# Two transformer blocks on one core: rotary rotations by transfers of rows instead of matmuls, and the mixers' rotation arithmetic on GpSimd

## The chip, the cores and the metric

One core of one Trainium2 chip. The metric is device microseconds of one execution. The engines are TensorE (PE), VectorE (DVE), ScalarE (ACT), GpSimd (POOL) and SyncE (SP), which issues most of the DMAs.

## What is computed

Two programs follow one another on a sequence of 256 tokens with 1024 features, both two layers deep and in fp32. The first block is a vision block with a context stream of another 256 tokens; the second ("mixer") has three kinds of attention between two feed-forward parts. Both turn some of their query and key rows by rotary angles:

```python
def apply_rope(x, cos, sin):            # first block: pairs (2i, 2i+1)
    x0, x1 = xf[..., 0], xf[..., 1]
    out = jnp.stack([x0 * cos - x1 * sin, x0 * sin + x1 * cos], axis=-1)

def partial_rope(x, cos, sin):          # mixer: rows i and i+8 of each head's first 16
    r1 = (x1 * c - x2 * s).astype(x.dtype)
    r2 = (x2 * c + x1 * s).astype(x.dtype)
    return jnp.concatenate([r1, r2, x[..., ROPE_DIM:]], axis=-1)
```

In the first block the grouped queries (8 heads) and keys are turned after their norm. In the mixer it is the 5 query heads of the selecting attention (`q_c`), its key `k_c`, the 4 index queries `q_i` and the index key `k_i`.

## The kernel before

Features lie on the 128 partitions, tokens along the free dimension. Each product of an activation with a weight is made of three fp32r matmuls (high part by high part, low by high, high by low). The weights come in 330-odd **pieces** of up to 1 MB through a ring of four buffers. ACT writes a piece's high part (`w_hi`, line 1750), DVE subtracts it to the low part in place (`ring_lo`, line 2267, called by `ahead`), PE reads both (lines 1258, 1301, 1395, 1504). Each function that adds to the plan appends an item to one list, and each engine walks this list in order and does what it has in every item; no engine changes its order at run time.

SP issues the pieces in order. Piece n goes out as soon as PE has begun piece n-3:

```python
if p.n >= RING:
    sp.wait_ge(piece_begun, p.n - RING + 2)
```

A rotation is an item `rope`. PE multiplies the chunk of 128 rows (64 for the index key and for the last query head) by a fixed matrix `rot1` or `rot2` of 0, 1 and -1 into a PSUM bank (line 1548, fp32). DVE then makes the product of that with the sine (line 2635), of the chunk with the cosine (line 2636) and the sum (line 2638), which raises `rope_ready`. Those who need it wait for this semaphore: PE's scores of the grouped and of the selecting attention (`pe_att`), PE's index scores (`pe_index`, line 1679), ACT's copies of keys (lines 1977, 2077).

There are 24 rotations, numbered through: 1 to 5 in layer 0 of the first block, 6 to 10 in its layer 1, then 7 in each layer of the mixer. In layer 0 of the first block the list alternates steps of attention (`att`), chunks of gate weights (`gates`) and pieces of the modulation weights (`mod`, line 1410). An attention step is: scores into the two S banks (line 1572), softmax on DVE out of these banks (line 2668; reciprocal line 2680), exponentials on ACT, the product with the reciprocal on POOL (line 2184), transposes on PE (line 1585), copies, values (line 1600). Half of the steps stand in the middle of a chunk's matmuls (`mids`). The scores of the next step wait until DVE has emptied both S banks. The head norm (`head_sums`, `head_spread`, DVE line 2624) precedes the rotations. In layer 0 rotation 3 stands between `head_spread` of the last chunk (pieces 23 and 24 just before it) and the attention step ahead of piece 25.

In the mixer the rotations stand among the matmuls of pieces 188 to 190 (layer 0) and 301 to 303 (layer 1), and the index scores among those of the piece after (`2f`, chunk 10).

## Time and profile before

| | |
|---|---|
| median of 3 runs | 2416.3 us (2415.94 to 2416.79) |
| the profiled execution | 2416.34 us |
| its span, first to last instruction | 2414.5 us |
| PE busy | 2393.6 us, 99% of the span |
| DVE, ACT, POOL busy | 64%, 51%, 17% |
| mean granted clock of PE | 0.999 |

A busy share is an average over stages. Rows of a timeline give start and length in us; the length of a matmul overlaps that of its neighbours, so the spacing of starts tells what one costs. Line numbers are those of the kernel before. "<-" in brackets names what ended the idle time before an instruction.

### The profile page before, as it was taken

The page shows a single profiled execution, that of the slowest core. Times are in us where ns is not written, and L with a number is a line of the kernel's source. Part 1 is how long each engine was busy: PE and PEld are TensorE (multiplying, and loading weights), DVE is VectorE, ACT ScalarE, POOL GpSimd, SP SyncE. Part 2 cuts the span into 40 slices and gives each one's busy share as a digit, 9 for nine tenths or more (in the row PEclk, how much of TensorE's full clock was granted, in tenths as well). Part 3 has the DMA queues.
Part 4 walks back from the last instruction along what each step waited for, and adds up shares of the span by engine and source line. Part 5 has one row for each costly group of instructions (what it writes and reads, how often), then busy time and mean ns, then how long its engine had stood idle before and what let it go on. Part 6 is the DMA issues. An engine that isn't in the chain of part 4 may idle for free.

```text
span 2414.5 us, 36498 instructions
## 1 busy us (share of the span) xinstructions
PE 2393.6 (99%) x14216; PEld 2036.5 (84%) x14216; DVE 1538.3 (64%) x2659; ACT 1219.4 (51%) x2268; POOL 405.0 (17%) x388
## 2 busy tenths in 40 slices
PE   8999999999999999999999999999999999999998
PEld 6766689888888877988888899898888889989887
DVE  5335455663455555677677777677767767767775
ACT  4344444322222546565565545665556554566554
POOL 0343322000001335100100100540010010154000
PEclk9999999999999999999999999999999999999999
DMA  6334423453444422455565553355565564436554
GB/s 280 132 114 158 157 88 122 159 169 135 157 165 141 157 89 95 150 192 176 194 212 181 172 184 128 123 193 192 170 208 180 176 195 151 151 112 200 190 175 137
DMA packets 88602, 389.92 MB, mean 161 GB/s; under 512 B 15024, under 2 KB 27600, under 8 KB 58352
## 3 DMA queue, kind: packets, MB, share of 16 engines
q1 hardware_dynamic: 81232, 356.07, 43.4%
q0 software_dynamic: 7200, 31.52, 3.8%
q8 instruction: 114, 1.87, 0.3%
q14 instruction: 56, 0.46, 0.1%
HBM read 386.52 MB, written 1.05 MB: 161 GB/s over the span
## 4 chain that ended last, share of the span: by engine, by line
PE 93%; DVE 3%; ACT 2%; POOL 1%; issue 1%; DMA 0%; DVEq 0%; SPq 0%; POOLq 0%; ACTq 0%
PE ps L1301 42%; PE ps L1258 38%; PE ps L1504 3%; PE ps L1572 2%; PE ps L1585 2%; PE ps L1600 2%; DVE ring_lo L2267 1%; PE ps L1395 1%; ACT logits L1989 1%; ACT w_hi L1750 1%; PE ps L1410 1%; POOL logits L2184 1%; PE ps L1548 1%; DMA x_res<-xt 0%; PE ps L1429 0%
## 5 line engine op out<-in xcount | busy, mean ns | idle before, releaser
L2267 DVE TENSOR_TENSOR ring_lo<-ring,w_hi 128x1024 fp32r<-128x1024 f32 (+4 forms) x708 | 781.8, 1129 | 200.1 <-ACT w_hi L1750 199.0
L1750 ACT ACTIVATE w_hi<-ring 128x1024 fp32r<-128x1024 f32 (+4 forms) x708 | 633.4, 944 | 280.1 <-PE ps L1258 186.7
L1301 PE MATMUL ps<-h_hi,w_hi 128*128 128x512 f32 x2144 | 527.2, 393 | 0.6 <-DVE h_hi L2440 0.3
L1301 PEld LDWEIGHTS ps<-h_hi,w_hi 128*128 128x128 f32 x2144 | 391.3, 188 | 76.6 <-issue 2.5
L1258 PE MATMUL ps<-h_hi,w_hi 128*128 128x256 f32 (+1 forms) x1520 | 410.6, 333 | 2.0 <-ACT arena L1879 1.2
L1258 PE MATMUL ps<-h_lo,w_hi 128*128 128x512 f32 (+1 forms) x976 | 325.5, 351 | 0.0
L1301 PEld LDWEIGHTS ps<-h_hi,ring_lo 128*128 128x128 f32 x2144 | 281.3, 191 | 14.5 <-DVE ring_lo L2267 0.9
L1301 PE MATMUL ps<-h_hi,ring_lo 128*128 128x256 f32 x2144 | 288.2, 282 | 0.0
L1258 PEld LDWEIGHTS ps<-h_hi,w_hi 128*128 128x128 f32 x1520 | 252.3, 190 | 37.6 <-issue 11.2
L1258 PE MATMUL ps<-h_hi,ring_lo 128*128 128x256 f32 (+1 forms) x1248 | 253.3, 338 | 0.3 <-DVE ring_lo L2267 0.3
L2509 DVE TENSOR_TENSOR prob_t<-ps,prob_t 128x256 f32<-128x256 f32 x260 | 109.7, 422 | 196.3 <-ACT prob_t L1902 196.0
L2140 POOL TENSOR_TENSOR logits<-logits 128x256 f32<-128x256 f32 (+1 forms) x65 | 67.6, 1040 | 991.0 <-ACT logits L1771 776.5
L1301 PE MATMUL ps<-hid_both,w_hi 128*128 128x512 f32 x880 | 226.2, 392 | 0.0
L1258 PEld LDWEIGHTS ps<-h_hi,ring_lo 128*128 128x128 f32 x1248 | 200.8, 189 | 28.4 <-issue 2.2
L2184 POOL TENSOR_SCALAR logits<-logits,stat 128x512 f32<-128x512 f32 (+2 forms) x140 | 167.9, 1211 | 261.4 <-DVE stat L2680 261.2
L1902 ACT ACTIVATE prob_t<-ps 128x256 f32<-128x256 f32 x260 | 98.1, 377 | 220.6 <-PE ps L1301 220.3
L1258 PEld LDWEIGHTS ps<-h_lo,w_hi 128*128 128x128 f32 x976 | 182.3, 189 | 23.5 <-DVE h_lo L2440 0.2
L1301 PEld LDWEIGHTS ps<-hid_both,w_hi 128*128 128x128 f32 x880 | 160.8, 188 | 30.9
L1989 ACT ACTIVATE logits<-logits,stat 128x512 f32<-128x512 f32 (+2 forms) x140 | 81.6, 584 | 140.4 <-DVE logits L2668 85.5
L1301 PE MATMUL ps<-hid_both,ring_lo 128*128 128x256 f32 x880 | 133.4, 282 | 0.0
L1301 PEld LDWEIGHTS ps<-hid_both,ring_lo 128*128 128x128 f32 x880 | 122.4, 191 | 5.7
L1928 ACT ACTIVATE prob_t<-prob_t 128x256 f32<-128x256 f32 x110 | 46.0, 418 | 105.3 <-DVE prob_t L2533 93.5
(301 smaller groups left out, 2934.0 us busy)
## 6 DMA issues: line engine op xcount, KB each, us to landing
ring<-w_ffn_in SPq DMA_DIRECT2D x132, 1024.0 KB, 4.9
ring<-w_ffn_out SPq DMA_DIRECT2D x96, 704.0 KB, 4.0
ring<-w_in SPq DMA_DIRECT2D x36, 1024.0 KB, 4.9
ring<-w_w_in SPq DMA_DIRECT2D x26, 1024.0 KB, 5.0
bias_t<-w_mod POOLq DMA_DIRECT2D x24, 1024.0 KB, 5.4
ring<-w_mod SPq DMA_DIRECT2D x16, 1024.0 KB, 6.0
ring<-w_up SPq DMA_DIRECT2D x16, 576.0 KB, 3.8
ring<-w_pab SPq DMA_DIRECT2D x8, 1024.0 KB, 4.9
```

Source lines behind the costliest of these rows:

```text
L1258: mm = pe.matmul(ps[fs[k].bank][:, at_col:at_col + n], (hi_w if wpart == "hi" else lo_w)[0:rows, at[k]:at[k] + P], hi if part == "hi" else ...
L1301: mm = pe.matmul(ps[f.bank][:, 0:cols], wt[:, at + q * P:at + q * P + P], both[:, 0:cols], start=left[q] == n, stop=left[q] == 1, skip_gro ...
L1504: mm = pe.matmul(ps[f.bank][:, 0:st["n"]], rows, wt[:, at:at + st["n"]], start=c == 0 and part == 0 and not low, stop=c == KC - 1 and low)
L1572: mm = pe.matmul(ps[f.bank][:, s2["at"]:s2["at"] + s2["nk"]], p["q"][a, s2["t"] * P:(s2["t"] + 1) * P], p["k"][a, k0:k0 + s2["nk"]], start ...
L1585: mm = pe.transpose(ps[f.bank][:, c * P:(c + 1) * P], logits[:, o:o + P], ident)
L1750: act.activation(w_hi[q.s % 2][:, h * n:(h + 1) * n], ring[q.slot][:, h * n:(h + 1) * n], ACT.Copy)\
L1902: act.activation(tmp[i][:, S:SQ], ps[f.bank][:, S:SQ], ACT.Copy).then_inc(half_out, 1)
L1989: act.activation(lg, lg, ACT.Exp, scale=-1.0, bias=stat[:, o:o + 1], accum_out=stat[:, 4 + o:5 + o])\
L2140: pool.tensor_tensor(sq_sum[:, o:n], sq_sum[:, o:n], sq[j % 2][:, o:n], ALU.add).then_inc(sq_added, 1)
L2184: pool.tensor_scalar(lg, lg, stat[:, 8 + (a % 2) * 2 + h:9 + (a % 2) * 2 + h], None, ALU.mult)\
L2267: dve.tensor_tensor(ring_lo[q.slot][:, c], ring[q.slot][:, c], plain(w_hi[q.s % 2][:, c]), ALU.subtract)\
L2509: dve.tensor_tensor(tmp[i][:, to:to + S], ps[f.bank][:, 0:S], tmp[i][:, S:SQ], ALU.add).then_inc(psum_taken[f.bank], 1)
```

## The change

The matrices `rot1` and `rot2` and all 24 matmuls go. In their place SP copies the partner rows of a chunk into a buffer (`turned_by`, `turned_by2`, two halves each) by DMA, from SBUF to SBUF: in the first block two transfers of 64 rows with a step of two, in the mixer two transfers of 8 rows for each head. The signs are in the sine table now. Each swap stands in SP's stream behind the load of a given piece (`plan.swaps`), waits until its chunk is written and until the rotation two before is done, since that one used the same half. The arithmetic stays on DVE in the first block, with a wait for the transfers; in the mixer it is on POOL, three operations with a wait between. In layer 1 of the first block and in the mixer the items have moved in the list too. `swap_clear` zeroes `turned_by2` once on DVE.

```diff
@@ -85,27 +85,20 @@
...
-    put("rot1", rot)
-    put("sin1", np.sin(ang).T[pair])
+    put("sin1", np.sin(ang).T[pair] * np.where(p % 2, 1, -1)[:, None])
-    put("rot2", rot)
...
-            sin[a] = sin[b] = np.sin(ang[i])
+            sin[a], sin[b] = -np.sin(ang[i]), np.sin(ang[i])
@@ -627,9 +623,20 @@
-        def rope(chunks, block, need=(), inside=False, bank=None):
-            return add("rope", block=block, need=need, tb=turned_by if block == 1 else turned_by2, inside=inside,
-                       chunks=[(b, a, low, fill(T_BANKS[i % 2] if bank is None else bank) if bank or not inside else linear(), count("rope")) for i, (b, a, low) in enumerate(chunks)])
+        def swap(chunk, block, need, later=0):
+
+            buf, at, low = chunk
+            n = count("swap")
+            moves = 2 if block == 1 or low else 4
+            t = dict(buf=buf, at=at, low=low, block=block, need=need, n=n, tb=turned_by if block == 1 else turned_by2,
+                     landed=count(f"swap_landed{n % 2}", 16 * moves))
+            plan.swaps.setdefault(len(plan.pieces) + 2 + later, []).append(t)
+            return t
+
+        def rope(*turns):
+            for t in turns:
+                count("rope")
+                add("rope" if t["block"] == 1 else "rope2", t=t, part=count("rope_part", 2) if t["block"] == 2 else None)
 
         def head_norm(chunks, root, kv=False, low=(0,) * 5):
@@ -831,12 +842,14 @@
                 some(unit, 2)
                 two_steps()
                 head_spread(hn, 0, 1)
+                turned = swaps(0, 1)
                 some(unit, 2)
                 two_steps()
                 head_spread(hn, 2, 3)
                 some(unit, 2)
                 two_steps(last=False)
-                rope(ropes[:2], 1, need=(hn["spread"][1],))
+                rope(*turned)
+                turned = swaps(2, 3, later=2)
                 add("keys_swap", n=1)
                 turn(unit)
                 unit = held_unit(2)
@@ -845,11 +858,12 @@
                 two_steps()
                 some(unit, 2)
                 head_spread(hn, 4)
-                rope(ropes[2:3], 1, need=(hn["spread"][2],), bank=T_BANKS[1])
+                rope(turned[0])
+                turned += swaps(4, later=1)
                 two_steps(last=False)
-                rope(ropes[3:4], 1, need=(hn["spread"][3],))
+                rope(turned[1])
                 two_steps()
-                rope(ropes[4:5], 1, need=(hn["spread"][4],))
+                rope(turned[2])
                 for _ in range(3):
                     some(unit, 2)
                     two_steps(last=False)
@@ -878,21 +892,25 @@
                 head_sums(hn)
                 next(nk[1])
                 head_spread(hn, 0, 1)
+                turned = swaps(0, 1)
                 g = attention([dict(na_pair(0, 0, 0, SQ), after=(feats["naq", 0], feats["nak", 0]))])
                 att(g)
                 run_all(nk[1])
                 head_spread(hn, 2, 3)
+                rope(*turned)
                 vals = values()
                 att(g)
+                turned = swaps(2, 3)
                 head_spread(hn, 4)
                 spread4 = plan.items[-1]
                 spread4["inside"] = True
                 next(vals)
                 plan.items[-1]["mids"] = {12: ("head_spread", spread4)}
-                among = {4 + 8 * i: rope([r], 1, need=(hn["spread"][i],), inside=True) for i, r in enumerate(ropes)}
+                rope(*turned)
+                turned = swaps(4)
                 tok("nav", w["w_nav"][l], 2, SLOT, 512, SQ, nav)
-                plan.items[-1]["mids"] = among
                 next(vals)
+                rope(*turned)
                 add("keys_swap", n=plan.counts["rope"] - 4)
                 g["steps"] += attention([na_pair(i, 0, 0, SQ) for i in range(1, 4)] + [gq_pair(i, 0, 0, SQ) for i in range(4)])["steps"]
                 att(g)
@@ -1034,8 +1052,11 @@
                     accs.append(fill(T_BANKS[h % 2]))
                     add("stick_acc", h=h, f=accs[-1], n=5 * l + h)
 
+            if l == 0:
+                add("swap_clear")
             run_all(chunks(0, fresh=plan.counts["h"], norm=defer()), chunks(1))
             add("y2_pad", after=fc(QI + 1))
+            turned_i = [swap(rows_of(QI + i), 2, fc(QI + i)) for i in range(2)]
             tok(f"vb{l}", w["vb2"][l], 2, 4 * 384, 384, S, vb2, scaled=True, n_out=330)
             add("kvup_load", l=l, before=kv_last[0])
             hn = head_norm([(feat2, CKV * S, S, v("g_kv", l), fc(CKV)), (feat2, KX * S, S, v("g_idx", l), fc(KX))], hroot2, True, (0, DH))
@@ -1043,23 +1064,34 @@
             t = chunks(2)
             next(t)
             head_sums(hn)
-            among(t, lambda: {10: [turned((feat2, QI * S, 0), 0, fc(QI))], 18: [turned((feat2, (QI + 1) * S, 0), 1, fc(QI + 1))]})
+            rope(turned_i[0])
+            turned_12 = swap(rows_of(12), 2, fc(12))
+            next(t)
+            rope(turned_i[1])
+            turned_13 = swap(rows_of(13), 2, fc(13))
             run_all(t)
             t = chunks(3)
             next(t)
+            rope(turned_12)
             head_spread(hn, 0, 1)
-            among(t, lambda: {13: [turned((feat2, 12 * S, 0), 1, fc(12))], 20: [turned((feat2, 13 * S, 0), 0, fc(13))]})
+            turned_key = swap(rows_of(KX, DH), 2, hn["spread"][1])
+            next(t)
+            rope(turned_13)
             run_all(t)
             t = chunks(4)
             kv = [fill(b) for b in (T_BANKS[0], T_BANKS[1], V_BANK)]
             kv_last[0] = kv[-1]
-            among(t, lambda: {8: [add("kvup", l=l, fs=kv, need=hn["spread"][1], inside=True)],
-                              16: [turned((feat2, KX * S, DH), 0, hn["spread"][1])]})
+            among(t, lambda: {8: [add("kvup", l=l, fs=kv, need=hn["spread"][1], inside=True)]})
+            rope(turned_key)
+            turned_c = swap((kc2, 0, 0), 2, kv[0])
             key_turned = plan.counts["rope"]
             add("key_twice", n=key_turned, k=count("key_twice"))
-            among(t, lambda: {8: [turned((kc2, 0, 0), 1, kv[0])], 16: [turned((feat2, QX * S, DH), 0, fc(QX))]})
+            next(t)
+            rope(turned_c)
+            turned_q = swap(rows_of(QX, DH), 2, fc(QX))
             run_all(t)
             among(feat(f"2f{l}", [(0, P, cols(5, 0, P))], [10], S, length=KC * P), lambda: {6: [index(0, 0, 1)], 16: [index(0, 2, 3)]})
+            rope(turned_q)
             t = chunks(5)
             among(t, lambda: {6: [index(1, 0, 1)], 16: [index(1, 2, 3)]})
             add("index_caps")
@@ -1173,6 +1205,19 @@
                                  first_src(half, i // 2, i % 2))\
                         .then_inc(first_landed[4 * half + i], 16)
 
+            def swap_rows(t):
+                sp.wait_ge(psum_taken[t["need"].bank], t["need"].taken)
+                if t["n"] > 2:
+                    sp.wait_ge(rope_ready, t["n"] - 2)
+                src, dst = t["buf"][:, t["at"]:t["at"] + S], t["tb"][:, t["n"] % 2 * S:(t["n"] % 2 + 1) * S]
+                if t["block"] == 1:
+                    for a in range(2):
+                        sp.dma_start(dst[a:P:2, :], src[1 - a:P:2, :]).then_inc(s_swap[t["n"] % 2], 16)
+                    return
+                for h in range(t["low"], P, DH):
+                    for a, b in ((0, 8), (8, 0)):
+                        sp.dma_start(dst[h + a:h + a + 8, :], src[h + b:h + b + 8, :]).then_inc(s_swap[t["n"] % 2], 16)
+
             first_mod(0)
             for p in plan.pieces:
                 if p.n == 2:
@@ -1186,6 +1231,8 @@
                         u = src.shape[1]
                         dst = dst.rearrange("p (u n) -> p u n", u=u)[:, :, a:a + src.shape[2]]
                     sp.dma_start(dst, src).then_inc(landed[p.slot], 16)
+                for t in plan.swaps.get(p.n, ()):
+                    swap_rows(t)
             for k in range(4):
                 sp.wait_ge(out_ready, 2 * k + 2)
                 sp.dma_start(out[:, 2 * k:2 * k + 2, :], arena[:, 2 * k * S:(2 * k + 2) * S].rearrange("p (c t) -> p c t", c=2))\
@@ -1539,14 +1583,6 @@
-
-            def pe_rope(st):
-                pe.wait_ge(s_tables, 16 * st["block"])
-                taken(*st["need"])
-                for buf, at, low, f, _ in st["chunks"]:
-                    room(f)
-                    pe.matmul(ps[f.bank][low:P, 0:S], cn(f"rot{st['block']}")[low:P, low:P], buf[low:P, at:at + S], start=True, stop=True)\
-                        .then_inc(psum_full[f.bank], 1)
@@ -2219,6 +2255,19 @@
                 pool.wait_ge(mg_hi_ready, n)
                 pool.tensor_tensor(at_T(mg2_lo, m, S), merged(0, m), plain(at_T(mg2_hi, m, S)), ALU.subtract).then_inc(mg_ready, 1)
 
+            def pool_rope(st):
+                t = st["t"]
+                low = t["low"]
+                pool.wait_ge(s_tables, 32)
+                taken(t["need"])
+                pool.wait_ge(s_swap[t["n"] % 2], t["landed"])
+                c, r = t["buf"][low:P, t["at"]:t["at"] + S], t["tb"][low:P, t["n"] % 2 * S:(t["n"] % 2 + 1) * S]
+                pool.tensor_tensor(r, r, cn("sin2")[low:P, :], ALU.mult).then_inc(rope_part, 1)
+                pool.tensor_tensor(c, c, cn("cos2")[low:P, :], ALU.mult).then_inc(rope_part, 1)
+                pool.wait_ge(rope_part, st["part"])
+                pool.tensor_tensor(c, c, r, ALU.add).then_inc(rope_ready, 1)
+                pool.wait_ge(rope_ready, t["n"])
+
             def pool_tables(st):
                 if st["n"] == 1:
                     pool.wait_ge(psum_full[st["after"].bank], st["after"].full)
@@ -2625,17 +2674,15 @@
                         .then_inc(psum_taken[f.bank], 1)
 
             def dve_rope(st):
-                b = st["block"]
-                dve.wait_ge(s_tables, 16 * b)
-                for f in st["need"]:
-                    taken(f)
-                for buf, at, low, f, n in st["chunks"]:
-                    c, t = buf[low:P, at:at + S], st["tb"][low:P, n % 2 * S:(n % 2 + 1) * S]
-                    full(f)
-                    dve.tensor_tensor(t, ps[f.bank][low:P, 0:S], cn(f"sin{b}")[low:P, :], ALU.mult).then_inc(psum_taken[f.bank], 1)
-                    link(dve.tensor_tensor(c, c, cn(f"cos{b}")[low:P, :], ALU.mult))
-                    taken(f)
-                    dve.tensor_tensor(c, c, t, ALU.add).then_inc(rope_ready, 1)
+                t = st["t"]
+                low, b = t["low"], 1
+                dve.wait_ge(s_tables, 16)
+                taken(t["need"])
+                dve.wait_ge(s_swap[t["n"] % 2], t["landed"])
+                c, r = t["buf"][low:P, t["at"]:t["at"] + S], t["tb"][low:P, t["n"] % 2 * S:(t["n"] % 2 + 1) * S]
+                link(dve.tensor_tensor(r, r, cn(f"sin{b}")[low:P, :], ALU.mult))
+                link(dve.tensor_tensor(c, c, cn(f"cos{b}")[low:P, :], ALU.mult))
+                dve.tensor_tensor(c, c, r, ALU.add).then_inc(rope_ready, 1)
 
             def dve_att(st):
                 steps, at = st["steps"], st["i"]
```

The order of SP in layer 0 of the first block, where pieces 22 to 28 go out (`w_mod` pieces carry modulation weights, `w_w_in` gate weights). Before:

```order
22 L1188 DMA ring<-w_mod 128x4x512 [waits piece_begun] x2
23 L1188 DMA ring<-w_w_in 128x2048 [waits piece_begun]
24 L1188 DMA ring<-w_mod 128x4x512 [waits piece_begun] x2
25 L1188 DMA ring<-w_w_in 128x2048 [waits piece_begun]
26 L1188 DMA ring<-w_mod 128x4x512 [waits piece_begun] x2
27 L1188 DMA ring<-w_w_in 128x2048 [waits piece_begun]
```

Now, from piece 19 on:

```order
21 L1233 DMA ring<-w_w_in 128x8x128 [waits piece_begun]
22 L1215 DMA arena<-arena 64x256 [waits psum5_taken]
23 L1215 DMA arena<-arena 64x256
24 L1215 DMA arena<-arena 64x256 [waits psum6_taken]
25 L1215 DMA arena<-arena 64x256
26 L1233 DMA ring<-w_mod 128x4x512 [waits piece_begun] x2
...
30 L1233 DMA ring<-w_mod 128x4x512 [waits piece_begun] x2
31 L1215 DMA arena<-arena 64x256 [waits rope_ready,psum5_taken]
32 L1215 DMA arena<-arena 64x256
33 L1215 DMA arena<-arena 64x256 [waits rope_ready,psum6_taken]
34 L1215 DMA arena<-arena 64x256
35 L1233 DMA ring<-w_w_in 128x2048 [waits piece_begun]
```

The transfers of rotations 1 and 2 (rows 22 to 25) stand between pieces 19 and 20, those of 3 and 4 (rows 31 to 34) between pieces 27 and 28.

DVE at rotation 3, from the gain of the last chunk on. Before:

```order
164 L2624 SCALAR_TENSOR_TENSOR arena<-arena,q_gain_scaled,ps 128x512 [waits psum5_full]
165 L2635 TENSOR_TENSOR arena<-ps,tables 128x256 [waits psum6_full,psum5_taken,tables_landed]
```

Now:

```order
164 L2673 SCALAR_TENSOR_TENSOR arena<-arena,q_gain_scaled,ps 128x512 [waits psum5_full]
165 L2683 TENSOR_TENSOR arena<-arena,tables 128x256 [waits rope_rows1_swapped,psum5_taken,tables_landed]
166 L2684 TENSOR_TENSOR arena<-arena,tables 128x256 [waits dve_chain]
167 L2685 TENSOR_TENSOR arena<-arena 128x256 [waits dve_chain]
168 L2316 TENSOR_TENSOR ring_lo_50<-ring,w_hi 128x1024 [waits w_hi_ready]
169 L2727 RECIPROCAL stat<-stat 128x2 [waits exp_ready]
170 L2715 TENSOR_SCALAR logits,stat<-ps 128x512 [waits psum5_full,psum3_full]
171 L2715 TENSOR_SCALAR logits,stat<-ps 128x512 [waits psum6_full,psum4_full]
```

The wait on a PSUM bank has become one on the transfers (`rope_rows1_swapped`); what stands behind it is as before.

POOL in layer 0 of the mixer, rotations 13 to 15 (the fifth, of 64 rows, is the index key's). It had nothing between the load of `kvup` and the gates; now:

```order
157 L2265 TENSOR_TENSOR arena<-arena,tables 128x256 [waits psum0_taken,rope_rows1_swapped,tables_landed,rope_ready]
158 L2266 TENSOR_TENSOR arena<-arena,tables 128x256
159 L2268 TENSOR_TENSOR arena<-arena 128x256 [waits rope_products_ready]
160 L2265 TENSOR_TENSOR arena<-arena,tables 128x256 [waits psum1_taken,rope_rows0_swapped,tables_landed,rope_ready]
161 L2266 TENSOR_TENSOR arena<-arena,tables 128x256
162 L2268 TENSOR_TENSOR arena<-arena 128x256 [waits rope_products_ready]
163 L2265 TENSOR_TENSOR arena<-arena,tables 64x256 [waits psum6_taken,rope_rows1_swapped,tables_landed,rope_ready]
```

Three operations a rotation, one rotation after another, have come to POOL.

## Rows read from the trace of the kernel before

**Rows 1.** The page's busy shares: busy us (share of the span) xinstructions.
```profile
PE 2393.6 (99%) x14216; PEld 2036.5 (84%) x14216; DVE 1538.3 (64%) x2659; ACT 1219.4 (51%) x2268; POOL 405.0 (17%) x388
```
**Rows 2.** The page's chain that ended last, share of the span by engine.
```profile
PE 93%; DVE 3%; ACT 2%; POOL 1%; issue 1%; DMA 0%; DVEq 0%; SPq 0%; POOLq 0%; ACTq 0%
```
**Rows 3.** Groups of instructions: line, engine, operation, tiles, count | busy us, mean ns.
```profile
L1548 PE MATMUL ps<-arena,tables 128*128 128x256 f32 x40 | 12.1, 388 | 0.5 <-ACT prob_t L1996 0.2
```
**Rows 4.** PE's timeline, mixer layer 0: start us, us, engine, line, operation, count.
```profile
1437.09 1.12 PE L1258 MATMUL ps<-h_hi,w_hi 128*128 128x256 f32 x8
1438.05 0.59 PE L1548 MATMUL ps<-arena,tables 128*128 128x256 f32 x2
1438.29 1.30 PE L1258 MATMUL ps<-h_hi,w_hi 128*128 128x256 f32 x8
1439.52 0.64 PE L1548 MATMUL ps<-arena,tables 64*64 64x256 f32 x2
...
1440.09 1.22 PE L1258 MATMUL ps<-h_hi,ring_lo 128*128 128x256 f32 x8
...
1441.96 0.49 PE L1679 MATMUL ps<-arena 64*128 64x128 f32 x4
```
**Rows 5.** PE's timeline, first block, layer 1, among the value weights.
```profile
854.29 0.39 PE L1504 MATMUL ps<-w_hi,h_lo 128*128 128x512 f32 x1
854.51 0.59 PE L1548 MATMUL ps<-arena,tables 128*128 128x256 f32 x2
854.76 0.58 PE L1504 MATMUL ps<-w_hi,h_hi 128*128 128x512 f32 x1
855.17 0.39 PE L1504 MATMUL ps<-w_hi,h_lo 128*128 128x512 f32 x1
```
**Rows 6.** PE's timeline, first block, layer 0, at rotation 3.
```profile
218.58 0.70 PE L1548 MATMUL ps<-arena,tables 128*128 128x256 f32 x2
219.21 1.13 PE L1572 MATMUL ps<-arena 64*128 64x512 f32 x4
...
223.61 1.13 PE L1572 MATMUL ps<-arena 64*128 64x512 f32 x4
```
**Rows 7.** DMA issues of the first 40 us: KB each, median us to landing.
```profile
vec<-vecs SPq DMA_DIRECT2D x1, 114.0 KB, 2.0
```
**Rows 8.** SP's timeline at pieces 26 and 27, and piece 27's landing.
```profile
216.74 1.23 SPq L1188 DMA_DIRECT2D ring<-w_mod  x2
...
ring<-w_mod SPq DMA_DIRECT2D x1, 1024.0 KB, 7.8
```
**Rows 9.** DVE's timeline, first block, layer 0: rotation 3, end of the softmax.
```profile
219.41 0.42 DVE L2635 TENSOR_TENSOR arena<-ps,tables 128x256 f32<-128x256 f32 x1
...
222.96 0.42 DVE L2693 COPY prob_t<-ps 128x256 f32<-128x256 f32 x1
```
**Rows 10.** ACT's timeline at piece 22, and PE's start on it.
```profile
194.23 2.00 ACT L1750 ACTIVATE w_hi<-ring 128x1024 fp32r<-128x1024 f32 x2 [0.84 <-DMA ring<-w_w_in]
...
196.64 0.49 PE L1258 MATMUL ps<-h_hi,w_hi 128*128 128x512 f32 x1
```
**Rows 11.** PE's first matmuls, its last long run, and the end (PE busy, granted clock).
```profile
3.16 7.34 PE L1203 MATMUL ps<-ones 128*128 128x128 f32 x40 [3.16 <-ACT silu_c L1755]
...
2403.73 2.17 PE L1203 MATMUL ps<-ones 128*128 128x128 f32 x18
...
2409.00:2414.00 5.00, 0.00 (x0) 0.77 0.57 210
```
**Rows 12.** POOL and DVE operations, ns min/median/max or busy us, mean ns; ACT's key copy.
```profile
L2191 POOL TENSOR_TENSOR x_res<-x_res,row x16: 719/735/854, 1482.9 to 2110.9; 128x256 f32<-128x256 f32 x16
...
L2212 POOL TENSOR_TENSOR logits<-logits 128x256 f32<-128x256 f32 x8 | 9.3, 1162 | 1.1
...
L2267 DVE TENSOR_TENSOR ring_lo<-ring,w_hi 128x1024 fp32r<-128x1024 f32 (+4 forms) x708 | 781.8, 1129 | 200.1 <-ACT w_hi L1750 199.0
...
1437.49 0.42 ACT L2077 ACTIVATE arena<-arena 64x256 f32<-64x256 f32 x1 [2.70 <-DVE arena L2638]
```

More of the change, by code:

```diff
@@ L57 @@
         (0, (("ident", P), ("sum_heads", 4 * 32), ("sum_kv", 2 * 32), ("row_sel", 8), ("vec_sel", 64), ("spread", 4 * P))),
-        (1, (("rot1", P), ("cos1", S), ("sin1", S), ("na_mask", 2 * S))),
-        (2, (("rot2", P), ("cos2", S), ("sin2", S), ("causal", 2 * S), ("strict", 384), ("adm_cap", 2 * S),
+        (1, (("cos1", S), ("sin1", S), ("na_mask", 2 * S))),
+        (2, (("cos2", S), ("sin2", S), ("causal", 2 * S), ("strict", 384), ("adm_cap", 2 * S),
              ("tri", 2 * S), ("later", P)))):
@@ L86, in constants @@
     put("spread", p[:, None] % 32 == np.arange(4 * P)[None] // DH)
-    rot = np.zeros((P, P))
-    rot[p[1::2], p[0::2]] = -1
-    rot[p[0::2], p[1::2]] = 1
-    put("rot1", rot)
     f = np.float32
@@ L96, in constants @@
     put("cos1", np.cos(ang).T[pair])
-    put("sin1", np.sin(ang).T[pair])
-    rot = np.zeros((P, P))
+    put("sin1", np.sin(ang).T[pair] * np.where(p % 2, 1, -1)[:, None])
     cos, sin = np.ones((P, S)), np.zeros((P, S))
@@ L154, in __init__ @@
         self.in_slot, self.held = [0] * RING, None
+        self.swaps = {}
     def add(self, kind, **kw):
@@ L332, in hybrid_kernel @@
         setup, silu_c_ready, amp_ready = sem("setup"), sem("silu_c_ready"), sem("amp_ready")
+        rope_part = sem("rope_products_ready")
+        s_swap = [sem(f"rope_rows{i}_swapped") for i in range(2)]
         x_done, squares, sq_added, rstd_ready = (sem(n) for n in ("x_done", "squares", "squares_added", "rstd_ready"))
@@ L738, in first_block, with swaps @@
             ropes = [(gk, 0, 0)] + [(gq, c * SQ, 0) for c in range(4)]
+            def swaps(*which, later=0):
+                return [swap(ropes[i], 1, hn["spread"][i], later) for i in which]
             def na_pair(i, q0, k0, nk):
@@ L1001, in index, with rows_of @@
                            n=[count("relu") for _ in hs], inside=True)
-            def turned(chunk, bank, *need):
-                return rope([chunk], 2, need=need, inside=True, bank=T_BANKS[bank])
+            def rows_of(c, low=0):
+                return (feat2, c * S, low)
             def among(tile, make):
@@ L1254, in product @@
                             for what, it in mids[at_mm] if isinstance(mids[at_mm], list) else [mids[at_mm]]:
-                                dict(sums=pe_sums, spread=pe_spread, att=pe_att, head_spread=pe_head_spread, rope=pe_rope, kvup=pe_kvup,
+                                dict(sums=pe_sums, spread=pe_spread, att=pe_att, head_spread=pe_head_spread, kvup=pe_kvup,
                                      index=pe_index, stick_z=pe_stick_z, unread=lambda u: between(dict(unread=u), 0))[what](it)
@@ L1487, in pe_tok @@
                 T, cols, n = st["T"], st["cols"], len(st["pieces"])
-                per, at_mm, mids = KC // n, 0, st.get("mids", {})
+                per = KC // n
                 for j, p in enumerate(st["pieces"]):
@@ L1716, in _ @@
                       half_row=pe_half_row, norm=pe_norm, norm_row=pe_norm, end=pe_norm, mod=pe_mod, mod_sum=pe_mod_sum, gv=pe_gv, mod_turn=pe_mod_turn, feat=pe_feat, gate_up=pe_gate_up, tok=pe_tok,
-                      head_sums=pe_head_sums, head_spread=pe_head_spread, rope=pe_rope, att=pe_att, merge1=pe_merge1,
+                      head_sums=pe_head_sums, head_spread=pe_head_spread, att=pe_att, merge1=pe_merge1,
                       merge2=pe_merge2, resid=pe_resid, kvup=pe_kvup, fox_bias=pe_fox_bias, index=pe_index, stick_z=pe_stick_z,
@@ L2237, in _ @@
             do = dict(resid=pool_stats, feat=pool_feat, half_chunk=pool_half_chunk, mod_load=pool_mod_load, na_bias=pool_na_bias, att=pool_att, merge1=pool_merge1,
-                      merge2=pool_merge2, tables=pool_tables, kvup_load=pool_kvup_load)
+                      merge2=pool_merge2, rope2=pool_rope, tables=pool_tables, kvup_load=pool_kvup_load)
             for st in items:
@@ L2756, in dve_fox_ls, with dve_swap_clear @@
                 dve.scalar_tensor_tensor(ls, small[:, 0:12], 0.0, small[:, 12:24], ALU.min, ALU.subtract).then_inc(f_ls, 1)
+            def dve_swap_clear(st):
+                dve.memset(turned_by2, 0.0)
             def dve_y2_pad(st):
@@ L2840, in _ @@
                       head_spread=dve_head_spread, rope=dve_rope, att=dve_att, y_split=dve_y_split, merge1=dve_merge1,
-                      merge2=dve_merge2, y2_pad=dve_y2_pad, fox_x=dve_fox_x, fox_ls=dve_fox_ls, fox_bias=dve_fox_bias, index=dve_index, index_caps=dve_index_caps,
+                      merge2=dve_merge2, swap_clear=dve_swap_clear, y2_pad=dve_y2_pad, fox_x=dve_fox_x, fox_ls=dve_fox_ls, fox_bias=dve_fox_bias, index=dve_index, index_caps=dve_index_caps,
                       index_round=dve_index_round, index_end=dve_index_end, stick_z=dve_stick_z, stick_ln=dve_stick_ln,
```

4 lines of the change are left out of this document (removed).

## The prediction

> **What bounds the kernel.** I read the busy shares first: the reader is to see that PE has work for 99% of the span [rows 1]. Then the chain that ended last: PE is 93% of it, no queue and no DMA more than a rounding [rows 2]. So a matmul that is taken out of PE's stream is worth its spacing there, and whatever is added is free until PE waits for it. Of PE's own stream I read the places of the 24 rotations (line 1548), then, at each, who in the changed order is late: DVE's, SP's and ACT's timelines. All sums are made against the profiled execution: 2416.34 us, of which 2414.5 are the span; the median of the runs is 2416.3, so no correction is needed. A measurement of this kernel tells about 0.2% (4.8 us) from no change.
>
> **What is removed: 24 fp32 matmuls.** One row carries 20 of them as 40 records, 12.1 us busy [rows 3]; busy time overlaps its neighbours, so I take the spacing of starts instead.
> - Mixers, 7 a layer. Eight matmuls take 0.96 us ahead of a rotation (1437.09 to 1438.05). The rotation holds 0.24 to the next start, and the next eight take 1.23 instead of 0.96: 0.51 in all. A rotation of 64 rows holds 0.57 [rows 4]. At the other places the first kind costs down to 0.43, as below. 5 x 0.46 + 2 x 0.63 (0.57 and a little behind it) = 3.6 a layer, 7.2 for two.
> - First block, layer 1, among the value weights: 0.25 to the next start, then 0.41 where the spacing is 0.22 [rows 5]: 0.43 each, 2.2 for five.
> - First block, layer 0: 0.63 from the start of a single rotation to the next work [rows 6], of which a part stays as the step from one kind of matmul to the next; 0.5 to 0.63 for three, 0.43 each for the pair. 2.6.
> Sum: 12.0 us off PE. The waits that DVE had for these matmuls go too; they cost nothing before, as DVE was not the bound.
>
> **What is moved to DMA and SP.** Each rotation in the first block is now two transfers of 64 rows, in the mixers two or four of 8 rows, in SP's stream behind the loads of given pieces. No row shows a transfer from SBUF to SBUF. From below: a small load on an empty queue lands after 2.0 us [rows 7]. From above: a load of 1 MB behind another took 7.8 us [rows 8]. So what matters is what lies ahead in the queue. I take 2 us on an empty queue, and with a load ahead, that load's landing and 0.4 us.
>
> *Layer 0, third rotation: the term that decides.* Its transfers stand on SP behind piece 27, that is behind two loads of 1 MB which go out at 216.74 and about 217.6, once PE begins pieces 23 and 24. The second of these lands 7.8 us after its issue, at 225.4 [rows 8]. DVE comes to this rotation right behind the last head's gain, and began it at 219.41; its S banks were free at 222.96, 3.55 us after that start [rows 9]. Now DVE waits there until 225.8, and in order behind it wait a ring_lo half, the reciprocal on which GpSimd's probabilities depend, and the softmax that empties the two S banks. PE's second scores behind it stood at 223.61 [rows 6], now at 223.0 with the rotation gone; the banks come free at 225.8 + 3.55 = 229.35. PE waits 6.4 us, with nothing else to do, since its stream is in order. The GpSimd work behind the reciprocal (3.1 us) ends about when PE comes to it, so I add nothing. Ends: 0 if the swap overtakes the load or the softmax is not needed so soon; 9 if the transfer takes another 2 us and the transposes wait too. I take 6.4: the queue row is near in kind. The fourth rotation's transfers landed meanwhile; the fifth's go out as soon as the third is done and have some 15 us; both cost nothing.
>
> *Layer 0, first two rotations.* Their four transfers (about 0.35 us of SP each, nearest row the loads' issue) wait for DVE's gain and stand ahead of pieces 20 to 22, which so go out some 1.3 us later. Piece 22 was on time to a hair: ACT waited for its landing, then split it (2.0 us) right up to PE's start at 196.64 [rows 10]. PE waits 1.1 us (0 to 2).
>
> *Layer 1.* SP holds piece 92 some 2.7 us for the fourth swap; it is needed 25 us later. DVE's rotations lie under the value weights' matmuls [rows 5], for which PE needs nothing of them: the scores that do come later. Free; if that cover were gone, a rotation's three operations of 0.42 [rows 9] cost 1.25 us each.
>
> *The clock.* In the last 5 us of the span PE has no instruction and the granted clock is 0.77, a mix of the two levels (1.2 and 2.4 GHz), so it falls when PE idles. The opening run of 40 small matmuls took 7.34 us, 0.184 each, where at full speed 18 took 2.17, 0.121 each: about 2.5 us lost to a slow start [rows 11]. A wait of 6.4 us should bring the lower level once: 2 us (0 to 2.5). TensorE: Matmul & The Clock Gate in the Trainium skill, part 1, says the same of idle stretches; by it alone the sum would be the same.
>
> **What goes to GpSimd: the mixers' arithmetic.** 14 rotations of three operations. A 128x256 operation has a median of 0.735 us in its quickest group and a mean of 1.162 in the slowest, which runs beside DVE's work [rows 12]. So 2.2 to 3.5 us a rotation. GpSimd had nothing here. The one in time is the index key's (fifth of a layer), for the index scores on PE at 1441.96 [rows 4], now 1438.1. By my estimate its rows are swapped at about 1432, behind the third rotation and piece 192's load; three operations and ACT's key copy (0.42) end between 1435 and 1436. Before, ACT waited 2.7 us for DVE at that copy [rows 12]; now no longer. I take 0; ends 0 and 2 a layer. SP's other waits here delay loads that have 5 us or more. DVE gets time free, worth nothing. The memset is 0.3 us of DVE, hidden.
>
> **Sum.** 2416.3 - 12.0 + 6.4 + 1.1 + 2.0 = 2413.8 us: no change that can be measured, for half the gain and more is given back at one wait.
>
> **Rivals.**
> - *The transfers are hidden everywhere* (the swap gets past the loads, or PE does not need DVE in that stretch). For it: the queue has 16 engines, DVE is busy for only 64% of the span [rows 1]. Against: the queue row [rows 8], in which a load behind another lands late; nothing shows a small transfer passing a large one. 2416.3 - 12.0 + 0.5 = 2404.8 us. Chance 0.22. With the wait there but only 3 us of it and no clock loss: 2408 to 2411; that is a part of the forecast's case, chance 0.13, and counts as faster.
> - *GpSimd becomes the bound in the mixers.* The third to fifth rotations follow one another there, and the key's swap waits for the third. If each operation waits for a whole DVE operation, 1.13 us in the ring_lo groups [rows 12], before its 0.735, a rotation is 5.6 us; with the third and fourth ahead of it running late too, the key is ready near 1445, and PE waits 6.8 us in each layer, with 2 us of clock each: 2413.8 + 17.6 = 2431 us, slower. It decides from about 1.2 us an operation on. Against: the slowest such group has a mean of 1.16 here, not 1.9, and DVE leaves gaps. SBUF — State Buffer in the Trainium skill, section "SBUF: two separate sides", says DVE with two SBUF inputs and GpSimd lock each other out for a whole instruction; by that rule taken at its worst the sum is this one; the trace agrees that both slow down, not that every operation does. Chance 0.05; of a partial form, or two more waits of the first kind, 2421 to 2425, 0.07.
> - *The change does not do what it says*: no; the order has no rotation on PE.
>
> **Numbers.** Forecast's own case, 2411.6 to 2421: 0.53. Faster by over 0.2%: 0.22 + 0.13 = 0.35. Within: 0.53. Slower by over 0.2%: 0.12. The range is 2405 to 2419: it takes in all but the last point of the hidden case, and of my own case all but a tail above 2419 that I put at 0.05; with the 0.12 above 2421, 0.17 and a little are left out.
>
> **What would show it.** Line 1548's rows gone; PE's matmul spacing unbroken at the 24 places. DVE idle about 6 us at the third rotation, released by a DMA onto arena, and PE idle about 6 us at the scores behind it: absent, the first rival. The granted clock below 1.00 in that 50 us. A wait of PE of about 1 us near 197. In the mixers GpSimd operations of 0.75 to 1.2 us, and no PE wait at the index scores; a wait there of over 1 us would be the second rival.

## The result and the profile after

| | before | after |
|---|---|---|
| median of 20 runs | 2416.28 us | 2420.82 us (2418.78 to 2423.1) |
| ratio | 1 | 1.0018, 95% interval 1.0012 to 1.0024 |
| profiled execution, its span | 2416.34, 2414.5 us | 2421.09, 2419.3 us |
| granted clock, mean | 0.999 | 0.997 |

The change made the kernel 4.5 us slower, 0.18%: small, but clear of the noise. The forecast was 2413.8 us, in a range of 2405 to 2419. The page's busy shares and chain of the kernel after, beside [rows 1, 2]: 6.9 us of matmuls are off PE's busy time and 43 us are new on GpSimd, yet the chain has lost two per cent of PE to DVE and DMA. Work left PE and waiting took its place.

```profile
PE 2386.7 (99%) x14168; PEld 2030.4 (84%) x14168; DVE 1530.6 (63%) x2618; ACT 1220.2 (50%) x2268; POOL 448.1 (19%) x430
...
PE 91%; DVE 4%; ACT 2%; DMA 1%; issue 1%; POOL 1%; SPq 0%; DVEq 0%; POOLq 0%; ACTq 0%
```

What PE waited for, in the kernel after (us in total, times, longest). Of these, the first, 2.3 us of the second, and the third are new.

```profile
PE ps L1608 <- DVE logits L2715: 7.0, 1, 7.0
...
PE ps L1305 <- ACT w_hi L1786: 2.5, 2, 2.3
...
PE ps L1715 <- ACT arena L2121: 1.3, 4, 0.5
```

I laid the two timelines of PE side by side, like instruction by like instruction, and read how far the later one is behind. The lead or lag changes in few places, and they add up (the opening differs from execution to execution: in the kernels below the lag 40 us in goes from -0.3 to +1.1):

| place (time before) | lag changes by, us | term on record |
|---|---|---|
| opening | +0.4 | none |
| near 197: PE waits (0.4 for piece 21, 2.6 for piece 22), then runs at the lower clock (1.5) | +4.5 | 1.1 |
| layer 0, rotations gone | -3.2 | -2.6 |
| second scores, 223.6: the wait | +7.1 | 6.4 |
| behind it: lower clock | +1.9 | 2.0 |
| layer 1, rotations gone | -1.9 | -2.2 |
| mixers, rotations gone (4.0 and 3.9) | -7.9 | -7.2 |
| mixers, waits at the index scores (1.5 and 1.5) | +3.0 | 0 |
| near 1599, an "issue" wait, 0.15 of it made up | +0.6 | none |
| near 2145 (in mixer_no_arith too) | +0.2 | none |
| sum | +4.7 | -2.5 |

**Place one, near 197.** SP's, ACT's and PE's timelines of the kernel after (start us, us, engine, line, operation, count). SP issues the four transfers first, 0.6 us each, and the three loads 2.5 us later. ACT has piece 22 at 197.88, where before it had it at 194.23 [rows 10]. 0.4 us of this is the opening's; 2.3 us is the first load going out later (185.58 for 182.90). The last microsecond lies in the loads' own transfer: their DMA packets begin 1.2 us behind the issue instead of 1.0, and take 10.6 us from the first to the last instead of 9.8.

```profile
183.08 2.46 SPq L1215 DMA_DIRECT2D arena<-arena  x4
185.58 1.14 SPq L1233 DMA_DIRECT2D ring<-w_mod  x2
186.76 0.71 SPq L1233 DMA_DIRECT2D ring<-w_w_in  x1
...
197.88 2.00 ACT L1786 ACTIVATE w_hi<-ring 128x1024 fp32r<-128x1024 f32 x2 [4.12 <-DMA ring<-w_w_in]
...
200.02 0.47 PE L1305 MATMUL ps<-h_hi,w_hi 128*128 128x512 f32 x1 [2.32 <-ACT w_hi L1786]
```

**Place two, rotation 3.** DVE's and PE's timelines. The gain ends at 223.5, the rows are there at 230.19, and the scores follow 3.9 us later, 0.4 us more than the forecast had; before, DVE went straight on [rows 9]. The rows' packets on SP's queue begin at 228.51, when the two loads ahead have all but ended (229.2).

```profile
230.19 0.42 DVE L2683 TENSOR_TENSOR arena<-arena,tables 128x256 f32<-128x256 f32 x1 [6.74 <-DMA arena<-arena]
...
234.10 2.08 PE L1608 MATMUL ps<-arena 64*128 64x512 f32 x4 [7.01 <-DVE logits L2715]
```

**The clock behind both.** Stretches of the kernel after: start:end, length, then busy us of PE, PEld, DVE, ACT and POOL, the granted clock, the DMA share and GB/s. After 2.3 idle us of PE, 200 to 203 runs at 0.58, and after 7 us, 234 to 238 at 0.50: the lower level (1.2 GHz), for 3.4 us and for 3.9 us of PE's work. That costs 1.5 and 1.9 us.

```profile
196.00:200.00 4.00, 1.71 (x16) 0.73 (x9) 1.73 (x2) 2.00 (x2) 0.00 (x0) 1.00 0.86 273
200.00:203.00 3.00, 2.98 (x8) 2.38 (x9) 1.74 (x8) 1.88 (x6) 1.83 (x2) 0.58 1.14 401
...
234.00:238.00 4.00, 3.90 (x12) 1.30 (x12) 2.19 (x4) 1.69 (x6) 2.23 (x3) 0.50 0.01 4
```

**The mixers.** DVE's timeline in layer 0 before, then DVE's, GpSimd's and PE's after. GpSimd's third operation on the compressed key and its first on the query take 1.78 and 1.61 us instead of 0.74, while the two ring_lo halves beside them take 2.89 us instead of 2.36, and the small operation behind them 0.76 instead of 0.28. It is that operation, through ACT, for which PE waits.

```profile
1442.62 2.36 DVE L2267 TENSOR_TENSOR ring_lo<-ring,w_hi 128x1024 fp32r<-128x1024 f32 x2 [0.65 <-ACT w_hi L1750]
1444.90 0.28 DVE L2785 TENSOR_SCALAR arena<-arena 128x128 f32<-128x128 f32 x1
...
1447.34 2.89 DVE L2316 TENSOR_TENSOR ring_lo<-ring,w_hi 128x1024 fp32r<-128x1024 f32 x2 [0.85 <-ACT w_hi L1786]
1450.15 0.76 DVE L2835 TENSOR_SCALAR arena<-arena 128x128 f32<-128x128 f32 x1
...
1446.56 0.73 POOL L2266 TENSOR_TENSOR arena<-arena,tables 128x256 f32<-128x256 f32 x1
1447.37 1.78 POOL L2268 TENSOR_TENSOR arena<-arena 128x256 f32<-128x256 f32 x1
1449.23 1.61 POOL L2265 TENSOR_TENSOR arena<-arena,tables 64x256 f32<-64x256 f32 x1
...
1451.43 1.35 PE L1715 MATMUL ps<-arena 64*128 64x256 f32 x4 [0.46 <-ACT arena L2121]
```

### The profile page after: what moved, and what is told of

Its sections match the earlier page's. It is cut to its first block, busy times and chain, and to the rows that moved or that the text cites. A ratio compares the mean times of both kernels' runs of the same rounds, so it can differ in the third digit from the quotient of the medians.

```text
span 2419.3 us, 36459 instructions
## 1 busy us (share of the span) xinstructions
PE 2386.7 (99%) x14168; PEld 2030.4 (84%) x14168; DVE 1530.6 (63%) x2618; ACT 1220.2 (50%) x2268; POOL 448.1 (19%) x430
## 4 chain that ended last, share of the span: by engine, by line
PE 91%; DVE 4%; ACT 2%; DMA 1%; issue 1%; POOL 1%; SPq 0%; DVEq 0%; POOLq 0%; ACTq 0%
PE ps L1348 41%; PE ps L1305 36%; PE ps L1548 3%; PE ps L1608 2%; PE ps L1636 2%; PE ps L1621 2%; DVE ring_lo L2316 2%; ACT w_hi L1786 1%; PE ps L1442 1%; POOL logits L2220 1%; PE ps L1457 1%; ACT logits L2025 1%; DMA ring<-w_w_in 0%; DMA x_res<-xt 0%; PE ps L1476 0%
```

## The experiments

The theory after the result has three parts: A, the places of the swaps in SP's stream make both waits of layer 0; C, GpSimd's arithmetic in the mixers, beside DVE's, makes the waits at the index scores; the rest is what the rotations were worth. Each run is compared with runs of the kernel before on its own chip: 2416.2 us for third_early, first_late, both_places and mixer_no_arith, 2416.36 for mixers_vector, gpsimd_late, after_landing and block1, 2416.35 for narrow_rows and rows_by_act.

### third_early: the swaps of rotations 3 and 4 behind piece 25

```diff
-                turned = swaps(2, 3, later=2)
+                turned = swaps(2, 3)
```

> The swaps of rotations 3 and 4 in layer 0 stand behind piece 25 instead of piece 27; all else is the change. Theory A (the swap's place in SP's stream behind two loads of 1 MB makes DVE late): the 7.0 us wait of PE at the scores and the 1.85 us of lower clock behind it go, 2420.8 - 8.9 = 2411.9 us (2411 to 2413), DVE finds the rows landed. Rival B (the softmax behind it would be late anyway, or swaps land slowly wherever they stand): 2415 us or more, a wait of 3 us or more stays at those scores.

Measured: 2411.66 us, ratio 0.9982 (0.9974 to 0.9991). Theory A. DVE's timeline: the rotation starts where the gain ends, with no wait.

```profile
223.33 0.75 DVE L2673 SCALAR_TENSOR_TENSOR arena<-arena,q_gain_scaled,ps 128x512 f32<-128x512 f32 x1 [4.16 <-PE ps L1582]
224.00 0.42 DVE L2683 TENSOR_TENSOR arena<-arena,tables 128x256 f32<-128x256 f32 x1
```

SP now waits before those swaps until DVE has done rotation 1; in that stretch it has nothing else to issue. With nothing ahead in the queue the rows' last packet has landed at 213.9, 1.0 us after the end of SP's last issue.

### first_late: the swaps of rotations 1 and 2 behind piece 22

```diff
-                turned = swaps(0, 1)
+                turned = swaps(0, 1, later=3)
```

(in layer 0 alone)

> The swaps of rotations 1 and 2 in layer 0 stand behind piece 22 instead of piece 19; all else is the change. Theory A (SP's 2.5 us of issuing and the transfers ahead of pieces 20 to 22 make piece 22 late): PE's wait of 2.3 to 2.6 us near 197 and its lower clock go, 2420.8 - 4.5 = 2416.3 us (2415.5 to 2417.5). Rival B (the piece is late for another reason, for instance because its bytes share the DMA engines with the swaps wherever they stand): at most 1.5 us gained, 2419.3 or more.

Measured: 2417.11 us, 1.0005 (0.9996 to 1.0014): 3.7 of the 4.5 us. Theory A. The wait shrinks from 2.3 to 0.7 us, and the clock stays up behind it:

```profile
200.00:204.00 4.00, 4.00 (x25) 2.57 (x24) 2.21 (x4) 1.01 (x4) 1.64 (x3) 1.00 1.06 405
```

The profiled execution is the slowest of this kernel's eleven (2419.69 us), for a reason in the mixers, which the edit does not touch. In layer 0 the two ring_lo halves take 3.43 us, not 2.89; PE then waits 1.0 us instead of 0.46 at the index scores, and the clock falls behind that:

```profile
1444.64 3.43 DVE L2316 TENSOR_TENSOR ring_lo<-ring,w_hi 128x1024 fp32r<-128x1024 f32 x2 [0.84 <-ACT w_hi L1786]
...
1452.00:1454.00 2.00, 2.00 (x9) 1.13 (x8) 1.90 (x4) 0.44 (x3) 0.00 (x0) 0.50 0.00 0
```

PE loses 3.0 us there instead of 1.5; in after_landing's profiled execution it is 3.0 in layer 0 and 2.0 in layer 1. So with the same mixers' program this place costs 3.0 us in one execution and up to 5.0 in another.

### both_places: the two edits together

> Both edits together. If the two waits are independent: 2420.8 - 8.9 - 4.5 = 2407.4 us (2406 to 2409), 0.37% faster than the kernel before. If one wait hides a part of the other, or a new wait comes up in its place: 2410 or more.

Measured: 2409.01 us, 0.9970 (0.9959 to 0.9982). The two edits alone took 9.2 and 3.7 us off the change's time, together 11.8, 1.1 less than their sum, at the upper edge of the independent case. That they do not add up is not shown: the two profiled executions, of this kernel and of the change, are 12.9 us apart. Half a microsecond of PE's wait near 197 stays, PE loses another half at the scores behind rotation 3, and the mixers' waits stay.

### narrow_rows: the same transfers with a thirty-second of the bytes

```diff
-                src, dst = t["buf"][:, t["at"]:t["at"] + S], t["tb"][:, t["n"] % 2 * S:(t["n"] % 2 + 1) * S]
+                w = S if t["n"] > 5 else 8
+                src, dst = t["buf"][:, t["at"]:t["at"] + w], t["tb"][:, t["n"] % 2 * S:t["n"] % 2 * S + w]
```

> The change, with the transfers of layer 0's five rotations 8 columns wide in place of 256 (so only 8 columns of those rotations are right): the same number of transfers of the same rows at the same places, a thirty-second of the bytes. Theory I (what costs at piece 22 is SP's time to issue four transfers, 0.6 us each, and at rotation 3 the place behind the load): both waits stay, 2.3 and 7.0 us, 2420.8 us (2420 to 2421.5). Theory Q (the 256 KB themselves hold the DMA engines): piece 22 comes 1.4 us sooner, which is the part of its lateness that SP's issues do not explain, the wait near 197 falls to 1 us, and rotation 3's rows land with the load: 2418 to 2419.5 us.

Measured: 2420.98 us, the same as the change. PE's longest wait on piece 22 is again 2.3 us, that at the scores 6.5. So the bytes of the rows cost next to nothing (rotation 3's rows are there at 229.81, 0.4 us sooner): what costs is that there are transfers, 0.6 us of SP each and ahead of the loads. SP's issues explain 2.3 us of piece 22's 3.3 (both less the 0.4 us by which all was late); the last one stays without a cause, only that it isn't the bytes.

### rows_by_act: rotation 3's transfers on ACT's queue

```diff
             def swap_rows(t):
+                if t["n"] == 3:
+                    return
...
+            def act_swap(st):
+                t = st["t"]
+                act.wait_ge(piece_begun, 27 - RING + 2)
+                act.wait_ge(psum_taken[t["need"].bank], t["need"].taken)
+                act.wait_ge(rope_ready, 1)
...
+                    act.dma_start(dst[a:P:2, :], src[1 - a:P:2, :]).then_inc(s_swap[t["n"] % 2], 16)
```

> The change, with rotation 3's two transfers issued by ACT on its own queue at about the same moment (after the same condition that lets SP issue pieces 26 and 27) instead of by SP behind these loads. Theory O (order within one queue: the rows wait for the loads ahead of them): they land within 2 to 3 us, DVE's wait of 6.7 us falls to 2 or less and PE's at the scores to 2 or less, some 2413.5 us (2412 to 2415). Theory S (the loads keep the shared DMA engines busy, whichever queue): the rows land hardly sooner, 2419 us or more.

Measured: 2420.15 us, 1.0017 (1.0008 to 1.0026). ACT's and DVE's timelines:

```profile
221.84 1.15 ACTq L2125 DMA_DIRECT2D arena<-arena  x2
223.10 2.00 ACT L1789 ACTIVATE w_hi<-ring 128x1024 fp32r<-128x1024 f32 x2 [2.49 <-issue]
...
229.06 0.43 DVE L2695 TENSOR_TENSOR arena<-arena,tables 128x256 f32<-128x256 f32 x1 [5.39 <-DMA arena<-arena]
```

Theory S, nearly whole: issued on a queue of their own, with 2 MB under way on SP's, the rows are there 6.1 us after the last of the two issues, 1.1 us sooner than in the change. PE's wait at the scores falls only to 4.8 us, and a new one of 0.7 us stands before it, since ACT's split now comes behind its two issues; PE's wait near 197, which the edit does not touch, was 3.0 us in this execution. The DMA packets show what the rows waited for: their first one moves at 226.35, 3.4 us after the last issue, when the first load's packets end (its last at about 226.6); then they move among the second load's and have landed at 228.56, before that load has (229.6). So this transfer waited for the load ahead of it on the other queue, but not for both. The Trainium skill, DMA: Bandwidth & Descriptors, section "Queues, rings and completion order", says that each DMA engine takes turns between the queues, packet by packet; by that rule the rows should have passed most of the 2 MB. The trace agrees from 226.35 on and not before; the measurement decides here, and why the rows did not start sooner stays open.

### mixer_no_arith: the three GpSimd operations on 1 column

```diff
-                pool.tensor_tensor(r, r, cn("sin2")[low:P, :], ALU.mult).then_inc(rope_part, 1)
-                pool.tensor_tensor(c, c, cn("cos2")[low:P, :], ALU.mult).then_inc(rope_part, 1)
+                r1, c1 = r[:, 0:1], c[:, 0:1]
+                pool.tensor_tensor(r1, r1, cn("sin2")[low:P, 0:1], ALU.mult).then_inc(rope_part, 1)
+                pool.tensor_tensor(c1, c1, cn("cos2")[low:P, 0:1], ALU.mult).then_inc(rope_part, 1)
...
-                pool.tensor_tensor(c, c, r, ALU.add).then_inc(rope_ready, 1)
+                pool.tensor_tensor(c1, c1, r1, ALU.add).then_inc(rope_ready, 1)
```

> The mixers' rotations keep their swaps, waits and three GpSimd operations, but each operation works on 1 column in place of 256, so the mixers' rotations are left out of the result. Theory C (the mixers give back 3.1 us because GpSimd's 256-column operations run late and hold up DVE's): PE's waits near 1451 and 2046 go, 2420.8 - 3.1 = 2417.7 us (2417 to 2418.5). Rival D (the swaps are what is late, by 0.62 us of SP for each transfer): the waits stay, 2420 us or more.

Measured: 2416.94 us, 3.9 less than the change where 3.1 were expected; the mixers' waits of up to 5.0 us under first_late would explain a gain above 3.1. PE's waits at the index scores are gone, and DVE's rows there are back to their lengths of before:

```profile
1446.62 2.36 DVE L2317 TENSOR_TENSOR ring_lo<-ring,w_hi 128x1024 fp32r<-128x1024 f32 x2 [0.85 <-ACT w_hi L1786]
1448.90 0.28 DVE L2836 TENSOR_SCALAR arena<-arena 128x128 f32<-128x128 f32 x1
```

The swaps with all their issuing time are still there: theory C, not D.

### mixers_vector: the mixers' arithmetic on DVE

```diff
-                add("rope" if t["block"] == 1 else "rope2", t=t, part=count("rope_part", 2) if t["block"] == 2 else None)
+                add("rope", t=t, part=count("rope_part", 2) if t["block"] == 2 else None)
...
-                low, b = t["low"], 1
-                dve.wait_ge(s_tables, 16)
+                low, b = t["low"], t["block"]
+                dve.wait_ge(s_tables, 16 * b)
```

(on top of both_places)

> As both_places (2409.0 us), and the mixers' rotation arithmetic on DVE in place of GpSimd, at the same places of the program. Theory C1 (PE's waits at the index scores come from GpSimd and DVE slowing each other, and DVE has the time): they go, 2409.0 - 3.0 = 2406.0 us (2405 to 2407). Rival (DVE, in order, now stands at each rotation until its rows land, and the weights' low halves behind it come late): new waits of PE, 2409 us or more.

Measured: 2413.02 us, 4.0 slower than both_places: the rival. DVE's timeline:

```profile
1436.34 0.43 DVE L2683 TENSOR_TENSOR arena<-arena,tables 128x256 f32<-128x256 f32 x1 [2.35 <-DMA arena<-arena]
1436.80 0.42 DVE L2684 TENSOR_TENSOR arena<-arena,tables 128x256 f32<-128x256 f32 x1
1437.26 0.43 DVE L2685 TENSOR_TENSOR arena<-arena 128x256 f32<-128x256 f32 x1
1437.61 2.35 DVE L2316 TENSOR_TENSOR ring_lo<-ring,w_hi 128x1024 fp32r<-128x1024 f32 x2
```

Nothing is slowed, but DVE stands 2.35 us for the rows of the compressed key, which nothing needs for long, and the ring_lo halves behind it begin at 1437.61, where both_places has them at 1434.65. PE waits 1.9 us, and 1441 to 1445 runs at a granted clock of 0.57. So DVE alone is no way out at these places of the program.

### gpsimd_late: the last two rotations of a mixer later on GpSimd

```diff
-            rope(turned_c)
...
-            rope(turned_q)
...
             run_all(t)
+            rope(dict(turned_c, need=fc(5)), dict(turned_q, need=fc(5)))
             add("index_round")
             tok(f"va{l}", w["va2"][l], 2, 4 * 384, 384, S, va2, scaled=True)
```

(on top of both_places)

> As both_places (2409.0 us), but GpSimd does the last two rotations of each mixer (the compressed key's and the query's) only after the last chunk of features is out of its bank, some 12 us later; nothing needs them sooner. Theory C1 (it is the overlap of just these operations with DVE's work for the index scores that costs 1.5 us in each layer): 2409.0 - 3.0 = 2406.0 us (2405 to 2407). Rival C2 (the slowing moves with the operations): a new wait of PE some 12 us later, 2408 us or more.

Measured: 2405.72 us (2405.52 to 2406.22), 0.9956 (0.9944 to 0.9969): 10.6 us faster than the kernel before and 15.1 faster than the change. GpSimd's timeline:

```profile
1463.01 0.74 POOL L2264 TENSOR_TENSOR arena<-arena,tables 128x256 f32<-128x256 f32 x1 [31.04 <-DVE arena L2546]
...
1467.24 1.71 POOL L2265 TENSOR_TENSOR arena<-arena,tables 64x256 f32<-64x256 f32 x1
1469.03 1.61 POOL L2267 TENSOR_TENSOR arena<-arena 64x256 f32<-64x256 f32 x1
```

The operations meet DVE's again, at up to 1.71 us each, but where PE does not need DVE at once. (They stand 30 us later, not 12 as the expectation has it.) So the 3 us are not a matter of GpSimd's load; they are that of six operations a layer in a bad place. The five runs lie within 0.7 us, where the change's twenty spread over 4.3; that fits a place whose cost differs between executions, but was not tested by itself.

### after_landing: SP waits for piece 22 before the first swaps

```diff
+                if p.n == 22:
+                    sp.wait_ge(landed[p.slot], p.landed)
                 for t in plan.swaps.get(p.n, ()):
```

(on top of both_places)

> As both_places (2409.0 us), but SP issues the first two rotations' transfers only once piece 22 has landed. If the 0.5 to 0.7 us that PE still waits near 197 come from these transfers' sharing the queue with piece 22, though they stand behind it: 2409.0 - 0.7 = 2408.3 us and no wait there. If not: 2409.0 or, if pieces 23 and 24 now come late, more.

Measured: 2409.55 us, no better than both_places; PE still waits 0.5 us near 197. The transfers behind the load are not the cause of this wait. Its cause was not found.

### block1: the first block alone

The kernel before, with the first block's swaps as in both_places:

```diff
+        def rope1(*turns):
+            for t in turns:
+                count("rope")
+                add("rope1", t=t)
...
-                rope(ropes[:2], 1, need=(hn["spread"][1],))
+                rope1(*turned)
+                turned = swaps(2, 3)
```

and so on for the other rotations of the block.

> The first block's rotations as in both_places, the mixers as in the kernel before (rotation matmuls on PE, arithmetic on DVE). By the drift of PE's stream in both_places the mixers there gain 7.8 us and give back 3.1 at the index scores and 0.8 near 1599: 2409.0 + 3.9 = 2412.9 us (2412 to 2414). By the terms on record (mixers 7.2 us, nothing given back): 2416.

Measured: 2411.9 us, 0.9982 (0.9973 to 0.9991). It splits both_places' gain of 7.2 us: the first block brings 4.5 us, and the mixers 2.7 (by the medians of two chips; between the two profiled executions it is 4.0), where on record they had 7.2.

## Why the prediction was wrong, by its own steps

- *What is removed, 12.0 us.* Right, a little low: 13.0. Spacing of starts was the right measure.
- *Layer 0, third rotation, 6.4 us, and the clock, 2.0.* Right in mechanism and size: 7.1 and 1.9. third_early shows the cause. The reason given, the place behind the load in the queue, was only a part: rows_by_act shows that another queue is hardly better, since there too the rows wait for a load.
- *Layer 0, first two rotations, 1.1 us (0 to 2).* **This step failed.** "About 0.35 us of SP each, nearest row the loads' issue" was the wrong row: each took 0.60 us, so 2.5 us in place of 1.3 stood ahead of the loads, and one more came from a cause not found. PE so fell 3.0 us behind instead of 1.1, and behind this wait too the clock fell, for 1.5 us more, where the sum had charged the clock for one wait alone: 4.5 us in all.
- *The mixers, 0 (ends 0 and 2 a layer).* **This step failed too**: 3.0 us in the change's profiled execution, up to 5.0 in others. The index key was indeed in time, as forecast; the slack was looked for at that rotation alone. What cost was the two rotations behind it, which nothing needs soon: they slowed DVE's work for the index scores. The rival of GpSimd named the right pair of engines but the wrong chain, the key's, and its partial form at 0.07 was left outside the range. SBUF — State Buffer in the Trainium skill, section "SBUF: two separate sides", says that such a pair of instructions excludes each other for a whole instruction; the lengths of 1.78 us for 0.74, beside DVE operations of about 1.2, lie within what that rule gives (0.74 and 1.2 at most).
- *Layer 1 free.* Right: 1.9 us gained, nothing lost.
- *The range.* The misses of 3.4 and 3.0 us, with 0.6 at rotation 3 and its clock, 0.6 near 1599, 0.4 in the opening and 0.2 near 2145, less 1.0 more removed, make 7.2 us (7.0 by the medians). Only the first of them lay outside its own ends (3.0 us by waiting against 2, and no clock for it at all); for the others the range took the ends one at a time and not together.

The wait near 1599 has "issue" as its releaser, so nothing that the profile shows. It is 0.70 us in every kernel here with rotations on GpSimd, mixer_no_arith among them, and absent in block1 and mixers_vector, which have none. Its cause was not tested.

## What to carry to other kernels

A small transfer put into a stream of loads has three prices: the issuing engine's time ahead of the next load, its own landing behind the loads in flight, and whatever stands in order behind the engine that waits for it. Give it a place where the queue has nothing to do, and let no engine on the path wait for it. And work moved to GpSimd can be paid by DVE where the two overlap: look at what PE needs of DVE in that stretch, not at how busy either is; the same operations 30 us later were free.

## What the runs showed of the hardware that was not expected

- A transfer of rows from SBUF to SBUF takes SP 0.595 us (64 rows of 1 KB) or 0.625 us (8 rows) to issue, against a median of 0.33 to 0.37 for the loads of weights. Groups of the kernel after, ns min/median/max:

```profile
L1219 SPq DMA_DIRECT2D arena<-arena x48: 624/625/777, 1416.6 to 2039.9; - x48
L1215 SPq DMA_DIRECT2D arena<-arena x20: 465/595/707, 183.1 to 867.7; - x20
```

- Its bytes do not matter to the time at this size (narrow_rows, 2420.98 against 2420.82 us), and the other queue brings its rows only 1.1 us sooner (rows_by_act).
- Idle times of PE of 2.3 us (the change) and 1.9 us (mixers_vector) were each followed by some 3.4 us at the lower clock level; one of 0.7 us (first_late, near 197) was not. Shorter is not safe: at the index scores a wait of 1.0 us was followed by it in first_late (0.50 from 1452 to 1454) and in layer 0 of after_landing (0.57 from 1441 to 1445), and was not in layer 1 of after_landing (1.00 from 2036 to 2040).
